# The mixers' merge and output matmuls in three rounded passes instead of full precision

## The chip, the cores and the metric

One core of one Trainium2 chip runs the whole kernel. The metric is the device time of one execution in microseconds (us).

## The reference

A decoder trunk of two layers on 256 tokens of width 1024, all in float32.

```python
for l in range(2):
    h = rmsnorm(x, norm_mix_g[l])
    z = h @ w_in[l]                        # split into the inputs of four branches and four gates
    y_a, y_b, y_c, y_d = gating(...), pool(...), rwkv7(...), ssd(...)      # each (256, 512)
    proj = einsum('btkc,kcd->btkd', [y_a, y_b, y_c, y_d], w_branch[l])
    merged = sum_k sigmoid(z_g[k]) * proj[k]
    x = x + merged @ w_out[l]
    h = rmsnorm(x, norm_ffn_g[l])
    x = x + (swiglu(h) if l == 0 else moe_swiglu(h))     # dense, or the top 2 of 8 experts
return rmsnorm(x, norm_final_g)
```

The branch `rwkv7` is a recurrence over the tokens, done in two pieces of 128 tokens, each with a triangular inverse by doubling.

## The kernel before, in words

All large weights come as one stream of chunks of 128x2048 floats (1 MB), each 16 tiles of 128x128. SyncE loads them in order into a ring of 7 slots in SBUF; a slot is loaded again when TensorE has counted its chunk in `chunks_used`. A layer's mixers have 19 chunks of input projections (`Z_UNITS`), 24 of the merge (`MERGE_CHUNKS`) and 4 of the output projection; then come 42 chunks of the dense feed-forward, or 42 for each of 8 experts.

A step of the merge has two gate chunks (h times the gate columns) and one branch chunk (`pj`, y of one branch times its projection). There are 8 steps, two a branch, in the order A, B, D, C. `sg` holds a sigmoid gate, `mg` the merged sum. The branch C (rwkv7) is a long chain of small matmuls on banks `m` with drains by VectorE and ScalarE between them. To keep TensorE busy meanwhile, the merge is cut in quarter chunks (4 tiles), and `SIDE` says how many quarters TensorE does before which stage of the chain: 8 before the lora products `cw`, 4 before `ss`, 8 before `bo`, 8 before `kt`, then for each piece of 128 tokens one at each of s1, s2, s3, at each T and X step of the 6 levels (two at X from level 2 on), one at U and one at O, then 4 before `mu` and 4 before `va`: 78 in all. `merge` does the other 18 quarters and the output. On VectorE `products` multiplies projection by gate, GpSimd adds into `mg` (L1362), and ScalarE computes the gates (`gates`, L1192). Each engine carries out its instructions strictly in the order of its own program, and waits on semaphores.

The branch chunks of C (steps 6 and 7) are the last two of the merge: they need y_C, which is ready after `mu`, `va`, a reciprocal (L1652) and five more operations (to L1661).

Two kinds of matmul occur. A full-precision one (`mm` on float32, L437) is issued as two instructions by TensorE. In the first 12 projections, the dense layer and the experts a product is done in three rounded passes (`three`): ScalarE copies the weights rounded into a buffer (`w_high`, L1201, L1213, L1246), VectorE subtracts that from the chunk and writes the rest over it in the ring (`ring_low`, L1700, L1713, L1790), and TensorE adds high x high, high x low, low x high. The normed h is split in the same way (`h_high` L1207, `h_low` L1707). Merge and output chunks and the C projections are full-precision.

The dense layer is a hardware loop of two turns of 14 chunks over gbanks in the order 0, 1, 2, 3, 0, 1, 2.

Of the kernel before, what the change touches and what calls it, by code (L numbers as in the profile page):

```python
# [48 lines left out]
RING = 7  # L49
# [9 lines left out]
NS = 12  # L59
MERGE_ORDER = [0, 1, 3, 2]  # L60
# [13 lines left out]
N_MIX = NZ + N_MERGE + N_OUT  # L74
# [14 lines left out]
for _name, _k in PP_LIST:  # L89
# [6 lines left out]
           ("off", LEVELS * P), ("count", 4 * T), ("reset", 4 * T), ("sel", H * P), ("slots", CAP), ("slot", 1)]  # L96
# [4 lines left out]
NCC = _n  # L101

# [60 lines left out]
def trunk(nc, x_in, stream, pp_in, cc_in, sw_in, rep_in, out):  # L163
    with ExitStack() as ctx:
# [6 lines left out]
        x = sb("x", [P, DT, T])  # L171
        h = sb("h", [P, DT, T])
        ring_at = -(-nc.sbuf_base // 32) * 32
        ring = sb("ring", [P, RING, CW])
        cc = sb("cc", [P, NCC])
# [7 lines left out]
        arena = sb("arena", [P, 28264])  # L183
# [34 lines left out]
        yA, yB, yC, yD = (tiles(i * 1024, 4) for i in range(4))  # L218
# [21 lines left out]
        seg1 = tiles(2048, H, P)  # L240
# [11 lines left out]
        wb = area(24168, 512)  # L252
        ub = area(24680, 512)
# [5 lines left out]
        oo = tiles(12840, 4)  # L259
# [3 lines left out]
        k2 = tiles(24168, 4)  # L263
# [3 lines left out]
        sg = area(25192, 1024).rearrange("p (b f) -> p b f", b=2)  # L267
        mg = tiles(26216, DT)

        def sg_of(step, i):  # L270
# [5 lines left out]
        gbanks = [0, 1, 2, 3, 0, 1, 2]  # L276
        gu = tiles(4096, FT)
        sil = tiles(11264, RING)
# [3 lines left out]
        h_high = part("h_high", 0, [DT, T])  # L282
        h_low = part("h_low", 2048, [DT, T])
# [39 lines left out]
        low_ready = sem("low_ready")  # L323
        v_seq = sem("v_seq")
# [10 lines left out]
            "hg_filled hg_high_ready hg_ready silu_tok hid_ready hid_turned eu_high_ready eu_ready y_ready zeroed back_filled back_drained h_split h_split_high gu_part").split()}  # L335
# [30 lines left out]
        def chunk0(l):  # L366
            return l * MIX1
# [13 lines left out]

        class Count:
# [17 lines left out]
        def _(sp):  # L400
# [5 lines left out]
            for s in range(RING):  # L406
                sp.dma_start(ring[:, s, :], stream[s]).then_inc(landed[s], 16)
                if s == 1:
                    sp.dma_start(sw[:, :], sw_in[0]).then_inc(layer_in, 16)
                    sp.dma_start(cc[:, first:NCC], cc_in[:, first:NCC]).then_inc(all_consts_in, 16)  # L410
                    sp.dma_start(rep[:, :], rep_in[0]).then_inc(layer_in, 16)
# [21 lines left out]
        def _(pe):  # L433
# [39 lines left out]
            def project(l, lo, hi):  # L473

                for n in range(lo, hi):
# [9 lines left out]
                    if name == "v":  # L485
# [7 lines left out]
                        for c in range(NCH):  # L493
                            for k in range(4):
                                tc = slice(c * P, (c + 1) * P)
                                last = three(gb(("v", c))[:, :], h_high[:, 4 * i + k, tc], h_low[:, 4 * i + k, tc],
                                             wh[:, k, :], wl[:, k, :], i == 0 and k == 0, i == 1 and k == 3)
                    else:
                        g_free(pe, l, (name, i))
                        for j in range(2):  # L500
                            for k in range(DT):
# [4 lines left out]
                                if n < NS:  # L506
                                    last = three(o, high[:, DT * j + k, :], low[:, DT * j + k, :], h_high[:, k, :], h_low[:, k, :],
# [4 lines left out]
                    if n == 1:  # L512
                        pe.wait_ge(layer_in, 32 * (l + 1))
                        pe.wait_ge(all_consts_in, 16)
# [6 lines left out]
            def mixer_d_rows(l):  # L521
# [20 lines left out]
                for i in range(4):  # L542
                    m_free(pe, l, f"row{i}")
                    for j in range(2):
                        hd = 2 * i + j
                        last = mm(mb(f"row{i}")[:, j * T:(j + 1) * T], cc[0:H, CC["sel"] + hd * P:CC["sel"] + (hd + 1) * P], d_cs)
# [197 lines left out]

            def merge_quarters(l, lo, hi):

                for n in range(lo, hi):
                    (step, unit), part = MERGE_CHUNKS[n // 4], n % 4
                    w = chunk(chunk0(l) + NZ + n // 4)
                    if unit < 2:  # L750
# [3 lines left out]
                        j = part // 2  # L754
                        for k in range(4 * (part % 2), 4 * (part % 2) + 4):
                            last = mm(gb(("gate", step, unit))[:, j * T:(j + 1) * T], w[:, DT * j + k, :], h[:, k, :],
                                      k == 0, k == DT - 1)
                    else:

                        branch = MERGE_ORDER[step // 2]  # L760
                        if part == 0:
                            if branch == 0:
                                pe.wait_ge(S["ya_ready"], NCH * (l + 1))
                            elif branch == 1:
                                m_done(pe, l, "b0")
                                m_done(pe, l, "b1")
                            elif branch == 2:
                                pe.wait_ge(S["yc_ready"], l + 1)
                            else:
# [1246 lines left out]
```

## Time and profile before

| what | value |
|---|---|
| median of 3 runs | 2276.28 us (2273.89 to 2279.42) |
| profiled execution, its own time | 2273.16 us |
| its span in the profile | 2271.3 us |
| TensorE busy | 2188.7 us, 96% |
| VectorE busy | 1426.5 us, 63% |
| ScalarE busy | 1060.5 us, 47% |
| mean granted TensorE clock | 0.977 of full |
| HBM traffic | 222 GB/s over the span |

Layer 0's mixers take from the start to 466 us, the dense layer 477 to 722, layer 1's mixers to 1183, the router and the experts the rest. A busy share is an average over all of these. An engine that waits shows as idle time, put down to the one that released it; the chain of waits walks back from the last instruction and tells which engine's work set the end.

### The profile page before, as it was taken

To read this page: it belongs to the slowest core of one execution; us is meant where nothing else is said; L and a number is where in the kernel's file an instruction comes from. 1 tells how busy PE (TensorE), PEld (TensorE's weight loads), DVE (VectorE), ACT (ScalarE), POOL (GpSimd) and SP (SyncE) were. 2 spreads that over 40 slices of the span, in tenths; PEclk is the share of its full clock that TensorE was granted. 3 is DMA by queue.
4 is the path that set the end of the run, shared out by engine and by line. 5 is a ranking of instruction groups with operands and counts; after the bars stand their busy time and mean duration, and the time that the engine had idled before them with its cause. 6 is when DMAs were issued, how large, how long until landed. Compare 5 with 4: busy or idle time off the path is not lost.

```text
span 2271.3 us, 31016 instructions
## 1 busy us (share of the span) xinstructions
PE 2188.7 (96%) x12120; PEld 1789.0 (79%) x12120; DVE 1426.5 (63%) x1355; ACT 1060.5 (47%) x898; POOL 43.8 (2%) x44
## 2 busy tenths in 40 slices
PE   7999999989998999999997999999999999999997
PEld 6988988889997988889876777777777777777775
DVE  3746331355644465533225888888888888888885
ACT  4423111133333332211113777777777777677773
POOL 0200000000000010000000000000000000000000
PEclk9999999999999999999996999999999999999998
DMA  7523212434544433322231999989898999899892
GB/s 304 184 93 130 75 56 70 170 135 178 185 184 150 149 132 110 111 75 75 75 148 47 347 348 349 368 326 366 328 368 339 356 349 346 347 351 366 329 366 101
DMA packets 69342, 504.66 MB, mean 222 GB/s; under 512 B 7696, under 2 KB 7952, under 8 KB 8208
## 3 DMA queue, kind: packets, MB, share of 16 engines
q1 hardware_dynamic: 68832, 500.57, 58.7%
q10 hardware_dynamic: 432, 2.95, 0.3%
q8 instruction: 61, 1.00, 0.2%
q14 instruction: 17, 0.14, 0.0%
HBM read 502.44 MB, written 1.05 MB: 222 GB/s over the span
## 4 chain that ended last, share of the span: by engine, by line
PE 96%; DVE 2%; ACT 1%; issue 0%; DMA 0%; SPq 0%; DVEq 0%; ACTq 0%
PE g L437 63%; PE m L437 30%; PE m L470 1%; PE m L932 1%; DVE h L1386 1%; DMA ring<-stream 0%; DVE rstd L1384 0%; DVE arena L1605 0%; ACT w_high L1201 0%; ACT L1040 0%; ACT arena L1037 0%; DVE h L1911 0%; DVE arena L1607 0%; DVE arena L1863 0%; ACT rms L1040 0%
## 5 line engine op out<-in xcount | busy, mean ns | idle before, releaser
L1790 DVE TENSOR_TENSOR ring_low<-ring,we_high 128x2048 fp32r<-128x2048 f32 x336 | 769.1, 2290 | 153.4 <-ACT we_high L1246 153.0
L1246 ACT ACTIVATE we_high<-ring 128x2048 fp32r<-128x2048 f32 x336 | 644.3, 1918 | 273.9 <-PE g L437 181.0
L437 PE MATMUL g<-we_high,hg_high 128*96 128x512 f32 x896 | 358.5, 400 | 10.3 <-DVE ring_low L1790 10.3
L437 PE MATMUL g<-ring_low,hg_high 128*96 128x512 f32 x896 | 353.9, 395 | 0.0
L437 PE MATMUL g<-we_high,hg_low 128*96 128x512 f32 x896 | 352.6, 394 | 0.0
L437 PE MATMUL g<-h,ring 128*128 128x256 f32 x1472 | 334.8, 383 | 0.0
L437 PEld LDWEIGHTS g<-h,ring 128*128 128x128 f32 x1472 | 277.3, 192 | 42.8 <-issue 7.1
L437 PE MATMUL g<-h_high,w_high 128*128 128x256 f32 x768 | 219.6, 286 | 26.8 <-DVE h_low L1707 24.7
L437 PE MATMUL m<-arena 128*128 128x128 f32 (+7 forms) x1832 | 234.0, 295 | 8.8 <-DVE arena L1605 5.8
L437 PEld LDWEIGHTS m<-arena 128*128 128x128 f32 (+3 forms) x1832 | 211.5, 186 | 29.5 <-issue 17.6
L437 PE MATMUL g<-h_high,ring_low 128*128 128x256 f32 x768 | 219.3, 286 | 0.0
L437 PE MATMUL g<-h_low,w_high 128*128 128x256 f32 x768 | 218.8, 285 | 0.0
L437 PEld LDWEIGHTS g<-we_high,hg_high 128*96 128x96 f32 x896 | 145.0, 162 | 70.8 <-DVE ring_low L1790 11.0
L437 PEld LDWEIGHTS g<-we_high,hg_low 128*96 128x96 f32 x896 | 144.6, 161 | 62.8
L437 PEld LDWEIGHTS g<-ring_low,hg_high 128*96 128x96 f32 x896 | 144.8, 162 | 59.1
L437 PE MATMUL m<-we_high,eu_high 128*96 128x512 f32 x448 | 177.3, 396 | 0.0
L437 PE MATMUL m<-we_high,eu_low 128*96 128x512 f32 x448 | 176.4, 394 | 0.0
L437 PE MATMUL m<-ring_low,eu_high 128*96 128x512 f32 x448 | 176.3, 393 | 0.0
L437 PE MATMUL g<-arena,ring 128*128 128x256 f32 x768 | 175.2, 385 | 0.0
L437 PEld LDWEIGHTS g<-h_high,w_high 128*128 128x128 f32 x768 | 147.7, 192 | 29.0 <-issue 28.9
L437 PEld LDWEIGHTS g<-arena,ring 128*128 128x128 f32 x768 | 145.9, 193 | 19.7 <-issue 0.3
L437 PEld LDWEIGHTS g<-h_low,w_high 128*128 128x128 f32 x768 | 147.6, 192 | 0.1
(242 smaller groups left out, 2209.6 us busy)
## 6 DMA issues: line engine op xcount, KB each, us to landing
ring<-stream SPq DMA_DIRECT2D x472, 1024.0 KB, 4.8
cc<-cc_in SPq DMA_DIRECT2D x1, 2352.5 KB, 15.7
sw<-sw_in SPq DMA_DIRECT2D x1, 1088.0 KB, 10.6
sw<-sw_in ACTq DMA_DIRECT2D x1, 1088.0 KB, 5.0
x<-x_in SPq DMA_DIRECT2D x1, 1024.0 KB, 4.8
out<-h ACTq DMA_DIRECT2D x1, 1024.0 KB, 3.9
rep<-rep_in SPq DMA_DIRECT2D x1, 768.0 KB, 17.2
rep<-rep_in ACTq DMA_DIRECT2D x1, 768.0 KB, 6.8
```

The source lines that it names most:

```text
L437: return pe.matmul(o, a, b, start=start, stop=stop, skip_group_check=True)
L470: last = pe.transpose(mb(stage)[:, i * P:(i + 1) * P], src, ident)
L932: last = pe.transpose(mbank[g % 2][:, j * CAP:(j + 1) * CAP], hid_tok[:, g % 2, j * P:(j + 1) * P], ident[0:CAP, 0:CAP])
L1246: A(we_high[n % 3][:, :], ring[:, slot, :], ACT.Copy).then_inc(high_ready, 1)
L1386: q.add(V.scalar_tensor_tensor(h[:, k, :], x[:, k, :], gain(k), rstd[:, :], ALU.mult, ALU.mult), done)
L1790: TT(ring_low[:, slot, :], ring[:, slot, :], we_high[n % 3][:, :], ALU.subtract).then_inc(low_ready, 1)
```

## The change

- All 28 merge and output chunks of a layer are done with `three`. A chunk is split by halves of 1024 columns: ScalarE rounds half a chunk (`z_highs`) into one of five half slots (`z_w`), VectorE subtracts it in the ring (`z_lows`), and TensorE waits in `halves` for `z_low_ready`. A half slot is free when TensorE has done the half five before (`half_free`, counted in `half_used` for first and `chunks_used` for second halves).
- ScalarE does `z_highs` inside `gates`, up to five halves ahead of the quarter at hand. VectorE has calls `z_lows(l, upto)` written between the steps of branch C, up to half 46, then two halves each in `products` 12 and 14, and the rest before the output drains.
- y of each branch and the merged sum are split as well: `y_split` and `y_lows`, `mg_high` and `mg_low`; the matmuls of `pj` wait for `y_low_ready`, those of `out` for `mg_low_ready`.
- The ring has 6 slots instead of 7. The dense layer is written out without a hardware loop and uses the banks 0 to 3 in turn.
- Buffers move: h_high has its own tensor, y_C lies in h, `sg` in `rep` (so layer 1's `rep` is loaded after the merge), `mg` partly in h. The tables `count`, `reset` and `sel` no longer stay in SBUF: pooling multiplies by a constant and by a small table `early` for the first 16 tokens, GpSimd writes `reset` with two memsets, `sel` becomes a broadcast column of the identity, and one scan becomes two.

```diff
-RING = 7
+RING = 6
+N_SLOTS = 5
+HALF = 1024
+        def half_free(eng, l, m, b):
+            at = 2 * (l * N_LATE + m) + b - N_SLOTS
+            if at >= 0:
+                before, n, half = at // (2 * N_LATE), at % (2 * N_LATE) // 2, at % 2
+                if half:
+                    eng.wait_ge(chunks_used, chunk0(before) + NZ + n + 1)
+                else:
+                    eng.wait_ge(half_used, before * N_LATE + n + 1)
@@ tensor: merge_quarters, merge
-                    w = chunk(chunk0(l) + NZ + n // 4)
+                    half, quarter = part // 2, part % 2
+                    wh, wl = halves(l, n // 4, half)      # waits for z_low_ready
...
-                            last = mm(gb(("gate", step, unit))[:, j * T:(j + 1) * T], w[:, DT * j + k, :], h[:, k, :],
+                            last = three(gb(("gate", step, unit))[:, half * T:(half + 1) * T], wh[:, quarter, k % 4, :], wl[:, quarter, k % 4, :],
+                                         h_high[:, k, :], h_low[quarter][:, k % 4, :], k == 0, k == DT - 1)
...
+                            pe.wait_ge(S["y_low_ready"], 2 * (4 * l + step // 2 + 1))
...
+                            if i == 0 and j == 0 and k % 2 == 0:
+                                pe.wait_ge(S["mg_low_ready"], 4 * l + kt // 2 + 1)
@@ tensor: the dense layer
-                with pe.Fori(0, FT // (2 * RING)) as i:
-                    for s in range(2 * RING):
+                for s in range(FT):
@@ scalar
+                act.wait_ge(S["ya_ready"], NCH * (l + 1))
+                y_split(l, 0)
                 side("cw")
...
+            def z_highs(l, upto):
+                while highs[0] < 2 * l * N_LATE + min(upto, 2 * N_LATE):
...
+                    act.wait_ge(landed[c % RING], 16 * (c // RING + 1))
+                    half_free(act, l, m, b)
+                    A(half_slot(l, m, b), half_ring(ring, l, m, b), ACT.Copy).then_inc(z_high_ready, 1)
             def gates(l, lo, hi):
+                for q4 in range(lo, hi):
+                    (step, i), part = MERGE_CHUNKS[q4 // 4], q4 % 4
+                    z_highs(l, q4 // 2 + N_SLOTS)
+                    if (step, i) == (6, 2) and part == 0:
+                        y_split(l, 2)
...
+                    if (step, i) == (2, 0):
...
+                        y_split(l, 1)
+                    if (step, i) == (4, 0):
...
+                        y_split(l, 3)
+                gates(l, SIDE_END, 12 * STEPS)
+                z_highs(l, 2 * N_MERGE + N_SLOTS)
+                for i in range(4):
+                    act.wait_ge(merged, 2 * STEPS * l + 13 + i)
+                    A(mg_high[:, 2 * i:2 * i + 2, :], mg[i], ACT.Copy).then_inc(S["mg_high_ready"], 1)
+                z_highs(l, 2 * N_LATE)
@@ vector: mixer_c, calls added between its steps
+                y_lows(l, 0)
+                z_lows(l, 5)            # before the difference L1527
+                z_lows(l, 7)            # before side cw
+                z_lows(l, 9)            # after cum_ready
+                z_lows(l, 10)           # after the ss drains
+                z_lows(l, 12)           # after the products of ss and bo
+                z_lows(l, 14)           # after the reciprocal L1581
+                z_lows(l, 16)           # after the bo drains, before side kt
+                    z_lows(l, SIDE_AT[f"s3{c}"][1] // 2 + 2)      # before the s drains
+                        z_lows(l, SIDE_AT[f"z{lv}{c}"][1] // 2 + 3)   # between the T and the X drains
+                        if (c, lv) == (1, 0):
+                            y_lows(l, 3)
+                z_lows(l, SIDE_AT["mu"][1] // 2 + 2)
+                z_lows(l, SIDE_AT["va"][1] // 2 + 3)      # before the products of mu and va
                 q.step(V.reciprocal(va[:, :, :], va[:, :, :]))
+                z_lows(l, SIDE_END // 2 + 5)
...
+                y_lows(l, 2)
+                z_lows(l, 46)
@@ vector: products and merge
                         g_done(dve, l, unit)
+                        if n in (12, 14):
+                            z_lows(l, 48 + (n - 12))
...
+                            if i == 1:
+                                for p in (n % 4 - 1, n % 4):
+                                    dve.wait_ge(S["mg_high_ready"], 4 * l + p + 1)
+                                    TT(mg_low[p][:, :, :], mg[p], mg_high[:, 2 * p:2 * p + 2, :], ALU.subtract).then_inc(S["mg_low_ready"], 1)
             def merge(l):
                 products(l, SIDE_AT["va"][1], 12 * STEPS)
+                z_lows(l, 2 * N_LATE)
```

## Rows read from the trace of the kernel before

**Rows 1.** The page: busy time of the engines, and chain by engine.
```profile
PE 2188.7 (96%) x12120; PEld 1789.0 (79%) x12120; DVE 1426.5 (63%) x1355; ACT 1060.5 (47%) x898; POOL 43.8 (2%) x44
...
PE 96%; DVE 2%; ACT 1%; issue 0%; DMA 0%; SPq 0%; DVEq 0%; ACTq 0%
```

**Rows 2.** Chain of waits, 395 to 482 us: start, duration, engine, line, count.
```profile
407.56 58.72 PE g L437 x272
```

**Rows 3.** Chain of waits, the dense layer, 480 to 722 us.
```profile
560.22 2.10 issue
562.32 80.87 PE g L437 x672
```

**Rows 4.** Groups of ScalarE by shape: tile, count, busy us, mean ns.
```profile
L1117 ACT ACTIVATE arena<-arena 128x1024 f32<-128x1024 f32 x2 | 2.1, 1043 | 0.0
```

**Rows 5.** Timelines by engine, before the recurrence: start, duration, instruction, idle before and releaser.
```profile
156.12 20.88 PE L437 MATMUL g<-h,ring 128*128 128x256 f32 x96
178.30 4.89 PE L437 MATMUL m<-arena,sw 64*128 64x256 f32 x24 [1.29 <-ACT arena L1115]
...
226.34 1.13 PE L437 MATMUL m<-arena 64*128 64x256 f32 x8 [1.40 <-DVE arena L1605]
...
943.00 1.13 PE L437 MATMUL m<-arena 64*128 64x256 f32 x8 [1.40 <-DVE arena L1605]
...
164.06 3.89 DVE L1527 TENSOR_TENSOR arena<-arena 128x3584 f32<-128x3584 f32 x1 [5.24 <-ACT arena L1059]
...
210.73 1.23 DVE L1585 TENSOR_TENSOR arena<-arena 128x1024 f32<-128x1024 f32 x1 [6.00 <-ACT small L1137]
211.87 1.22 DVE L1587 TENSOR_TENSOR arena<-arena 128x1024 f32<-128x1024 f32 x1
...
224.05 0.69 DVE L1605 TENSOR_TENSOR arena<-m,cc 128x512 f32<-128x512 f32 x1 [4.52 <-PE m L437]
...
163.23 0.60 ACT L1059 ACTIVATE arena<-g 128x512 f32<-128x512 f32 x1 [6.07 <-PE g L437]
```

**Rows 6.** Timeline of VectorE, a level with two side quarters.
```profile
367.57 0.69 DVE L1628 TENSOR_TENSOR arena<-m,arena 128x512 f32<-128x512 f32 x1 [3.73 <-PE m L437]
```

**Rows 7.** Timeline of TensorE: rounded and full-precision matmuls in turn.
```profile
750.62 0.27 PE L437 MATMUL g<-h_high,ring_low 128*128 128x256 f32 x1
750.83 3.62 PE L437 MATMUL m<-h,sw 128*8 128x256 f32 x16
754.38 0.39 PE L437 MATMUL g<-h_high,w_high 128*128 128x256 f32 x1
754.60 0.28 PE L437 MATMUL g<-h_low,w_high 128*128 128x256 f32 x1
...
1421.01 0.45 PE L437 MATMUL g<-we_high,hg_high 128*96 128x512 f32 x1
1421.30 0.39 PE L437 MATMUL g<-ring_low,hg_high 128*96 128x512 f32 x1
```

**Rows 8.** Timelines by engine, the end of the merge in layer 0.
```profile
466.10 3.62 PE L437 MATMUL m<-arena,cc 128*128 128x256 f32 x16
...
408.38 6.55 DVE L1652 RECIPROCAL arena<-arena 128x1024 f32<-128x1024 f32 x1 [5.95 <-ACT arena L1179]
...
403.08 0.60 ACT L1192 ACTIVATE arena<-g 128x512 f32<-128x512 f32 x1 [1.15 <-POOL arena L1362]
```

**Rows 9.** Windows: length, TensorE busy (instructions), granted clock, DMA share, GB/s.
```profile
470.00:472.00 2.00, 0.00 (x0) 0.94 0.29 123
...
480.00:482.00 2.00, 2.00 (x11) 0.50 0.00 0
482.00:484.00 2.00, 2.00 (x19) 1.00 0.00 0
```

**Rows 10.** Experts: SyncE's issues in a timeline, and issue to landing.
```profile
1401.29 8.67 SPq L417 DMA_DIRECT2D ring<-stream  x4
...
ring<-stream SPq DMA_DIRECT2D x67, 1024.0 KB, 4.8
```

More of the change, by code:

```diff
@@ L743, in _, with halves @@
             ys = [yA, yB, yC, yD]
+            def halves(l, m, b):
+                pe.wait_ge(z_low_ready, 2 * (l * N_LATE + m) + b + 1)
+                return half_slot(l, m, b), half_ring(ring_low, l, m, b)
             def merge_quarters(l, lo, hi):
@@ L1399, in mixer_d_decay @@
                 q.step(V.tensor_scalar(d_abs, d_dt, ahead[0:H, 0:1], -1.0, ALU.mult, ALU.mult))
-                q.step(V.tensor_tensor_scan(d_cs, cc[0:H, CC["reset"]:CC["reset"] + T], d_abs, 0.0, ALU.mult, ALU.add), S["cs_ready"])
+                for c in range(NCH):
+                    tc = slice(c * P, (c + 1) * P)
+                    ins = V.tensor_tensor_scan(d_cs[:, tc], cc[0:H, CC["ones"]:CC["ones"] + P], d_abs[:, tc], 0.0, ALU.mult, ALU.add)
+                    (q.step(ins, S["cs_ready"]) if c else q.add(ins, v_seq))
             def mixer_d_conv(l):
@@ L1659, in mixer_c, with z_lows, y_lows @@
                     m_done(dve, l, f"cg{i}")
+                z_lows(l, 44)
                 q.step(TT(oo[:, :, :], oo[:, :, :], bv[:, :, :], ALU.add))
-                q.step(TT(yC[:, :, :], oo[:, :, :], gg[:, :, :], ALU.mult), S["yc_ready"])
+                for i in range(2):
+                    two = slice(2 * i, 2 * i + 2)
+                    q.add(TT(yC[:, two, :], oo[:, two, :], gg[:, two, :], ALU.mult), S["yc_ready"])
+                y_lows(l, 2)
+                z_lows(l, 46)
+            def z_lows(l, upto):
+                while lows[0] < 2 * l * N_LATE + min(upto, 2 * N_LATE):
+                    n = lows[0] - 2 * l * N_LATE
+                    m, b = n // 2, n % 2
+                    lows[0] += 1
+                    dve.wait_ge(z_high_ready, lows[0])
+                    TT(half_ring(ring_low, l, m, b), half_ring(ring, l, m, b), half_slot(l, m, b), ALU.subtract).then_inc(z_low_ready, 1)
+            lows = [0]
+            def y_lows(l, branch):
+                for i in range(2):
+                    dve.wait_ge(S["y_high_ready"], 2 * (4 * l + MERGE_ORDER.index(branch)) + i + 1)
+                    two = slice(2 * i, 2 * i + 2)
+                    TT(y_low[branch][:, two, :], (yA, yB, yC, yD)[branch][:, two, :], y_high[:, two, :], ALU.subtract).then_inc(S["y_low_ready"], 1)
             def products(l, lo, hi):
```

241 lines of the change are left out of this document (135 added, 106 removed).

## The prediction

> **What bounds the kernel now.** I read the page first: TensorE is busy 96% of the span, and the chain that ended last runs through it for 96% [rows 1]. So the question is how fast TensorE's work is and who can make it wait. The changed matmuls are the merge and output chunks: 28 chunks of 16 weight tiles in each of two layers, 896 tiles. Today a tile is a full-precision product of two instructions; in the longest run of them in the chain of waits 272 take 58.72 us, 0.216 each, 0.432 a tile [rows 2]. The dense stage already does three rounded passes: 672 instructions in 80.87 us, 0.1203 each, 0.361 a tile [rows 3]. The saving is 0.071 us a tile: 0.29 us a quarter chunk (1.73 to 1.44), and 64 us for all 896 if nothing else waits.
>
> By the Trainium skill (TensorE: Matmul & The Clock Gate, Back-to-back issue gap) a matmul of 256 columns follows the last after 109 ns; a tile would then take 0.33 us, and the saving be 94 us. The trace has 0.1203, so the row is used.
>
> **What is added.** Each of 56 half chunks a layer now needs a rounding copy on ScalarE and a subtraction on VectorE, of 128x1024 each. Nearest rows: 1.04 us on ScalarE [rows 4], 1.23 on VectorE, where the next one starts 1.14 after the last [rows 5]. That is 64 us of VectorE and some 55 of ScalarE a layer; the y and merged tiles add twelve pairs of 128x512 at 0.69 and 0.60 [rows 5]. In total VectorE has room (63% busy over the span), but each engine works in the order of its code, and the new instructions stand between links of the chain. So I follow layer 0 in three stretches. Layer 1 is the same 716.66 us later (226.34 and 943.00) [rows 5].
>
> **Stretch 1, from the last projection to the recurrence** [all from rows 5]. TensorE ends the projections at 163.0 (156.12 and 32 instructions) and today goes straight on with merge work; 28 quarters of it cover VectorE's preparation. After the change the first quarter waits: evacuation to 163.8, two roundings of y to 165.0, first rounding of weights 166.0, first subtraction 167.3. Idle 4.3. VectorE does y_lows(0) and five z_lows before its difference: 171.9 instead of 164.1; then 3.9 and 5.6 of mixing (to 181.5), tanh and sigmoid, and the lora matmuls start at 182.4 instead of 178.30. From there VectorE is the chain, in the order of its code: w_log scaled at 185.4, scan and sums 5.9, two z_lows, k2 2.6, the ss drain 1.3, one z_low, 3.6 for bonus, marker and products (202.3), two z_lows behind ScalarE's root and rounding (205.1), reciprocal 6.6, two z_lows, kk 1.2: 215.2. Today it is at this point at 210.73, after 6.00 us of waiting; that wait hides the other half of what is added. The five operations up to ab_ready take 5.9: 221.1; bonus drains 1.3. Then z_lows(16): ScalarE makes halves 14 and 15 only in its side "kt", after ab_ready and two drains, so their subtractions end at 226.9, and two products put the first drain of n (L1605) at 228.5 instead of 224.05. TensorE's pair of matmuls behind it comes at 230.7 instead of 226.34, after 6.4 us idle. Four quarters there give back 1.15; the clock (below) takes 1.8. Balance +5.0 us.
>
> **Stretch 2, the recurrence.** In a level with two side quarters VectorE has nothing to do for 3.73 us between draining T and draining X [rows 6]. With quicker quarters that gap is some 3.1 us, and 1.5 where a level has one quarter. One or two subtractions (1.2 or 2.4) are put into it; where two meet the short gap they are late by 0.8, which the next quarter hides. ScalarE waits only for halves used before its own step. So here TensorE stays the bound: 38 quarters save 10.9. y_lows(3), at level 0 of the second chunk, adds 1.3 to a short gap; I charge 1.0. If this cover were gone, a subtraction on the chain would cost its 1.2.
> Changing between rounded and full-precision matmuls: around the dt product (8 weight columns) the rounded instruction is followed after 0.21, the sixteen take 3.55 and the first rounded one is followed after 0.22, against 0.12, 3.46 and 0.12: +0.28 a round trip. After the expert transposes (128 wide) the first rounded one is followed after 0.29 instead of 0.23: +0.06 [rows 7]. With 40 interruptions a layer the bounds are 0 and 11 us; the weights here are wide like the transposes, so I take 0.06, 2.4 us. Balance -7.5.
>
> **Stretch 3, the end of the merge.** Today the va matmuls end at 407.56; eight quarters before them give 2.3: 405.2. On VectorE three z_lows stand before the products of step 5, so the gate (6,0), today at 403.08 behind GpSimd's sum, comes at 405.2; the gate, a rounding, the table load and two roots (0.6, 1.0, 1.3, 1.6) put the reciprocal at 409.6, today 408.38 [rows 8]. Halves 42 and 43 are subtracted only behind its 6.55: at 417.3 and 418.5. TensorE has finished half 41 at 413.8: idle 3.5. Next, ScalarE rounds y_C behind the gate (7,1) and half 48, which both wait for the end of half 43; then come y_lows(2) and half 44: 4.7 idle. Today TensorE reaches pj 6 at 424.8 without a wait; that cover is what goes. Halves 46 and 47 are subtracted only in products(12), which waits for all of chunk 22: 2.0. Halves 48 and 49 stand behind mg_low 0 and 1, these behind ScalarE's half 52, which needs the slot of half 47: 4.8. Half 50 stands behind mg_low 2 and 3: 1.2. From 417.3 on, 14 halves of 2.89 give 457.8, the four later waits 12.7, three clock drops 5.4: 475.9. Today 466.28. Balance +9.6.
>
> **The clock.** TensorE's last matmul before the norm ends at 469.7 [rows 8]. The granted clock was 0.94 in 470 to 472, 0.50 (1.2 GHz) in 480 to 482, when it had been back at work since 477.26, and 1.00 (2.4 GHz) from 482 [rows 9]. At 1.2 GHz 256 columns take 0.213 us instead of 0.1203. I take 4.1 us low, which costs 1.8 us an idle. Today only the norms and the router have such gaps; the short idles of 1.29 and 1.40 us in rows 5 brought no drop. I take a drop for each idle of 3.5 us or more: the one that counts in stretch 1 (before 167.3 another is hidden by the wait for 182.4) and three in stretch 3. Bounds: none, 7.2 us a layer less; all at the length of 477.26 to 482, 1 us a layer more.
>
> **The rest.** Unrolling the dense stage removes the 2.10 us at its loop's turn [rows 3]. The ring of six: in the experts a slot is issued every 2.9 us (three periods in 8.67) and landing takes 4.8 [rows 10]; ScalarE runs three chunks ahead, so a chunk has three periods, 8.7 us, instead of four: nothing, and about one period once if that margin failed. Half chunks free a slot with their second half, as a chunk does today. The smaller constants and their extra transfer land before anyone waits; GpSimd's two reset memsets and its rewritten pooling run long before they are asked for; rep for layer 1 is fetched behind the merge and used in layer 1; the broadcast identity column in place of "sel" and the split scan keep their counts: each nothing, at most 1 us.
>
> **Sum.** A layer: 5.0 - 7.5 + 9.6 = +7.1; two, less 2.1: +12.1. Against the profiled execution's own 2273.16 (span 2271.3) this is 2285.3. The median of the runs shown is 3.1 higher, so 2288.
>
> **Rivals.** (A) TensorE stays the only bound. For it: 96% busy, and VectorE idle for 3.73 us of each long level. All 64 us and the 2.1: 2210. Against: the waits of stretches 1 and 3 follow from the order of the code. Chance 0.10. The Trainium skill (Perfetto Trace Analysis, Identifying the Most-Contended Engine) says to relieve the engine with the highest occupancy; followed without looking at the order, that is this rival, and the rows of stretch 2 agree with it, those of 1 and 3 do not.
> (B) The same waits, but the clock stays up (14.4 less) and half of the four later idles of stretch 3 is absorbed (12.7 less): 2261. For it: these idles are near 4 us, where today's drops have over 7. Against: each is longer than the 2.3 us from 469.7 to 472. Chance 0.27, between 2245 and 2279.
> (C) On the other side: each round trip between precisions costs the 0.28 of the dt row; 80 times 0.22 more is 17.6: 2306. Its point of decision is 0.09 a trip: from there the change costs time even with the clock up all through (7.1 less 7.2 and 1.05 a layer, and 40 times 0.03). For it: rows 7. Against: no such loss into 128 columns. Chance 0.10.
> Forecast 0.53, its own range 2279 to 2300.
>
> **Numbers.** Within 0.2% of 2276.3 (2271.7 to 2280.9) a measurement of this kernel cannot tell from no change. Faster: A and two thirds of B, 0.29; same 0.14, the rest of B and the forecast's lower edge; slower 0.57. Range 2250 to 2308: it leaves out A and the far ends.
>
> **What would show it.** In the chain of waits, pieces of VectorE and ScalarE in 163 to 231 and 413 to 456, where today almost only TensorE stands. TensorE idle 3 to 5 us before the first merge quarter, before pj 6 and before out 0, released by ring_low or y_low, with a granted clock of 0.50 behind it. A level of two side quarters and one shorter by 0.9 us. A dense stage without its 2.10. I am wrong if the first drain of n stays within 2 us of today's, or if out 0 follows pj 7 without a gap.

## The result and the profile after

The changed kernel takes 2281.96 us (median of 13 runs, 2281.71 to 2287.89), the kernel before 2274.52 (13 runs of its own, 2270.68 to 2279.61): a ratio of 1.003, with a 95% interval of 1.0021 to 1.0039. It is slower by some 7 us. The profiled execution has a span of 2280.6 us, 9.3 longer, and its mean granted TensorE clock is 0.961 instead of 0.977.

The page first, its lines on busy time and the chain. TensorE is busy for 44 us less than in [rows 1], VectorE for 136 us more and ScalarE for 121 more. The chain no longer runs through TensorE alone: its share fell from 96% to 55%, with gaps that the profile can't follow.

```profile
PE 2145.0 (94%) x13016; PEld 1790.1 (78%) x13016; DVE 1562.3 (69%) x1495; ACT 1181.5 (52%) x1033; POOL 49.3 (2%) x56
...
PE 55%; DVE 4%; issue 1%; ACT 1%; POOL 0%; DVEq 0%; ACTq 0%
```

Next the waits of TensorE over the span (engine and line, what it waited for, us in total, times, longest). The first and the fourth line are new.

```profile
PE g L480 <- DVE ring_low L1778: 39.2, 12, 4.9
PE g L480 <- DVE h_low L1838: 24.0, 3, 9.3
PE m L480 <- ACT arena L1073: 12.6, 3, 7.8
PE m L480 <- ACT arena L1185: 12.3, 2, 6.3
```

Two of these waits stand ahead of the recurrence: the one ahead of the first merge quarter, which waits for the first subtracted half, and the one ahead of the score matmuls, which wait for a bank that ScalarE drains at L1185. Timelines of the kernel after, layer 0, with the instructions that answer to [rows 5] (last evacuation on ScalarE, halves and first drain of n on VectorE, TensorE):

```profile
162.23 0.60 ACT L1095 ACTIVATE arena<-g 128x512 f32<-128x512 f32 x1 [6.07 <-PE g L480]
163.76 4.84 ACT L1228 ACTIVATE z_w<-ring 128x1024 fp32r<-128x1024 f32 x5
...
164.84 5.77 DVE L1778 TENSOR_TENSOR ring_low<-ring,z_w 128x1024 fp32r<-128x1024 f32 x5
226.87 0.68 DVE L1698 TENSOR_TENSOR arena<-m,cc 128x512 f32<-128x512 f32 x1
...
180.89 4.89 PE L480 MATMUL m<-arena,sw 64*128 64x256 f32 x24 [1.60 <-ACT arena L1153]
230.27 3.79 PE L480 MATMUL m<-arena 64*128 64x256 f32 x16 [6.03 <-ACT arena L1185]
```

These 16 score matmuls are two groups of eight. In the kernel before, the first group ran at 223.85 and the second, the line at 226.34 in [rows 5], waited for VectorE's first drain of n. In the kernel after, both stand behind ScalarE's drain, and the second group starts at 232.11 (after, then the first group before, each group seen by itself):

```profile
232.11 1.95 PE L480 MATMUL m<-arena 64*128 64x256 f32 x8
```
```profile
223.85 1.09 PE L437 MATMUL m<-arena 64*128 64x256 f32 x8
```

The end of the merge, the same view of TensorE and VectorE, against [rows 2, 8]. TensorE stands still ahead of half 42 (412.39), of the branch chunk of step 7 (434.89) and of the first output chunk (445.83); ahead of the first branch chunk of C at 424.47 it waited 4.61 as well. The last addition to x comes at 471.86.

```profile
412.39 0.38 PE L480 MATMUL g<-h_high,z_w 128*128 128x256 f32 x1 [3.59 <-DVE ring_low L1778]
424.47 0.58 PE L480 MATMUL g<-y_high,z_w 128*128 128x256 f32 x1 [4.61 <-DVE ring_low L1778]
434.89 0.39 PE L480 MATMUL g<-y_high,z_w 128*128 128x256 f32 x1 [2.04 <-DVE ring_low L1778]
445.83 0.58 PE L480 MATMUL g<-mg_high,z_w 128*128 128x256 f32 x1 [4.92 <-DVE ring_low L1778]
451.42 0.39 PE L480 MATMUL g<-mg_high,z_w 128*128 128x256 f32 x1 [0.47 <-DVE ring_low L1778]
...
404.52 6.55 DVE L1754 RECIPROCAL arena<-arena 128x1024 f32<-128x1024 f32 x1 [4.86 <-ACT arena L1217]
471.86 0.69 DVE L1823 TENSOR_TENSOR x<-g,x 128x512 f32<-128x512 f32 x1 [4.88 <-PE g L480]
```

Windows behind two of these idles (length, TensorE busy with its instructions, weight loads, VectorE, ScalarE, GpSimd, granted clock, DMA share, GB/s). TensorE is back at work all through them, at half the clock (1.2 GHz), as in the first line at work of [rows 9].

```profile
424.47:429.00 4.53, 4.53 (x21) 4.53 (x22) 1.08 (x1) 0.00 (x0) 0.00 (x0) 0.50 0.02 4
446.00:450.00 4.00, 4.00 (x19) 4.00 (x20) 3.87 (x6) 1.26 (x2) 0.00 (x0) 0.50 0.00 0
```

With the same marks in both traces the whole difference can be laid out. The marks are the first matmul of a layer, the last evacuation of its projections, the second group of its score matmuls (226.34 before, 232.11 after), the end of the O matmuls of the second piece, and the last addition to x.

| stretch, us | before | after | change | predicted |
|---|---|---|---|---|
| layer 0, start to last evacuation | 163.23 | 162.23 | -1.0 | 0 |
| 1, to the second group of score matmuls, layer 0 / 1 | 63.11 / 63.11 | 69.88 / 70.16 | +6.8 / +7.0 | +5.0 each |
| 2, the recurrence, layer 0 / 1 | 163.68 / 163.71 | 153.08 / 152.92 | -10.6 / -10.8 | -7.5 each |
| 3, the end of the merge, layer 0 / 1 | 76.28 / 76.28 | 86.67 / 86.55 | +10.4 / +10.3 | +9.6 each |
| norm, dense layer, norm | 271.05 | 267.04 | -4.0 | -2.1 |
| layer 1, first matmul to last evacuation | 142.54 | 143.72 | +1.2 | 0 |
| router, experts, final norm | 1088.31 | 1088.35 | 0.0 | 0 |
| span | 2271.3 | 2280.6 | +9.3 | +12.1 |

### The profile page after: what moved, and what is told of

It reads as the page before. It is cut to its first block, busy times and chain, and to the rows that moved or that the text cites. A ratio compares the mean times of both kernels' runs of the same rounds, so it can differ in the third digit from the quotient of the medians.

```text
span 2280.6 us, 33009 instructions
## 1 busy us (share of the span) xinstructions
PE 2145.0 (94%) x13016; PEld 1790.1 (78%) x13016; DVE 1562.3 (69%) x1495; ACT 1181.5 (52%) x1033; POOL 49.3 (2%) x56
## 4 chain that ended last, share of the span: by engine, by line
PE 55%; DVE 4%; issue 1%; ACT 1%; POOL 0%; DVEq 0%; ACTq 0%
PE g L480 33%; PE m L480 21%; DVE ring_low L1778 1%; PE m L968 1%; PE m L513 0%; DVE arena L1754 0%; DVE arena L1672 0%; ACT z_w L1228 0%; DVE h L1467 0%; DVE h L2040 0%; DVE arena L1992 0%; DVE small L1994 0%; DVE y_low L1787 0%; DVE ring_low L1919 0%; DVE small L1455 0%
## 5 line engine op out<-in xcount | busy, mean ns | idle before, releaser
L480 PE MATMUL g<-we_high,hg_high 128*96 128x512 f32 x896 | 358.6, 400 | 10.3 <-DVE ring_low L1919 10.3
L480 PE MATMUL g<-h_high,ring_low 128*128 128x256 f32 x1280 | 366.2, 286 | 0.0
L480 PE MATMUL m<-arena 128*128 128x128 f32 (+7 forms) x1832 | 239.8, 302 | 20.4 <-ACT arena L1185 12.3
L480 PEld LDWEIGHTS g<-h_high,ring_low 128*128 128x128 f32 x1280 | 249.7, 195 | 0.0
L480 PEld LDWEIGHTS g<-ring_low,hg_high 128*96 128x96 f32 x896 | 144.8, 162 | 59.1
L1228 ACT ACTIVATE z_w<-ring 128x1024 fp32r<-128x1024 f32 x112 | 115.8, 1054 | 127.5 <-PE g L480 127.5
L1778 DVE TENSOR_TENSOR ring_low<-ring,z_w 128x1024 fp32r<-128x1024 f32 x112 | 132.4, 1220 | 53.1 <-ACT arena L1210 39.5
L480 PE MATMUL g<-h_high,z_w 128*128 128x256 f32 x512 | 153.1, 299 | 15.0 <-DVE ring_low L1778 15.0
```

Of the source, the lines that this page charges most:

```text
L480: return pe.matmul(o, a, b, start=start, stop=stop, skip_group_check=True)
L1228: A(half_slot(l, m, b), half_ring(ring, l, m, b), ACT.Copy).then_inc(z_high_ready, 1)
L1778: TT(half_ring(ring_low, l, m, b), half_ring(ring, l, m, b), half_slot(l, m, b), ALU.subtract).then_inc(z_low_ready, 1)
```

## The experiments

In what follows "after" is the changed kernel; each ratio is against runs of the kernel before on the same chip. A time "below after" compares medians of different chips, on which the kernel before has medians of 2274.5, 2276.5, 2278.7 and 2275.8 us, so such a difference is uncertain by a few us; by the ratios it is 26 us instead of 26.5 in the first experiment, for instance, and 19 instead of 16 in the one with two passes.

**The order at the end of the merge.** Nothing is computed differently; small instructions of VectorE and ScalarE change places.

```diff
 vector, mixer_c
                 side("mu", "va")
+                z_lows(l, 43)
 ...
+                z_lows(l, 45)
                 y_lows(l, 2)
-                z_lows(l, 46)
+                z_lows(l, 48)
 vector, products
-                        if n in (12, 14):
-                            z_lows(l, 48 + (n - 12))
 ...                                       # n == 13, ahead of mg_low and behind it
+                                    z_lows(l, 50)
+                                    z_lows(l, 52)
 scalar
-                    if (step, i) == (6, 2) and part == 0:
-                        y_split(l, 2)
+                    if (step, i) == (7, 1):          # behind its sigmoid
+                        y_split(l, 2)
-                gates(l, SIDE_END, 12 * STEPS)
+                gates(l, SIDE_END, 12 * STEPS - 2)   # mg_high 0 and 1 next, then the rest, then 2 and 3
```

> The changed kernel with another order of the small instructions in the end of each layer's merge, nothing else: half 42 is subtracted while VectorE waits for the square roots; the split of the recurrent mixer's output is issued by ScalarE right behind the last gate and not behind one more rounding; halves 44 to 49 and 50, 51 are subtracted in VectorE's free time ahead of the wait that they are needed at; the first two roundings of the merged tiles come ahead of two roundings of weights. Theory (stretch 3 is lost to waits that the order makes): TensorE's idles of 4.6, 2.0 and 4.9 us ahead of the last two projections and the first output chunk go, the projection of the recurrent mixer starts at 419.9 instead of 424.5, and the last add of x comes about 11.5 us earlier in each layer: 2282 - 23 = 2259 us. Rival (the waits only stand in for a chain of reciprocal, affine, split and products that would end last anyway, and the clock falls as before): at most the 4.6 us a layer, 2273 us. Rival (the stretch is paid in TensorE time, not in waits): no change, 2282 us.

Measured: 2255.46 us (2254.82 to 2257.70, 6 runs), ratio 0.9915 (0.990 to 0.993). That is 26.5 below after, a little more than the theory's 23. TensorE's timeline of this kernel has two idles left in the stretch; branch chunk 7 and the first output chunk (at 436.25, without an idle) follow at once. From the va matmuls (400.67) to the last addition to x it takes 59.26 us, in after 73.49 (398.37 to 471.86).

```profile
400.67 1.89 PE L480 MATMUL m<-arena,cc 128*128 128x256 f32 x8
...
414.68 0.39 PE L480 MATMUL g<-h_high,z_w 128*128 128x256 f32 x1 [0.75 <-DVE ring_low L1782]
422.21 0.55 PE L480 MATMUL g<-y_high,z_w 128*128 128x256 f32 x1 [4.40 <-issue]
436.25 0.36 PE L480 MATMUL g<-mg_high,z_w 128*128 128x256 f32 x1
```

TensorE's own time over the two stretches tells idles and clock apart (same columns as the windows above: length, TensorE busy, weight loads, VectorE, ScalarE, GpSimd, granted clock, DMA share, GB/s; after first, then this kernel). The same 419 matmuls keep it busy for 57.85 us and for 53.92. So of the 14.2 us, 10.3 are idles, and 3.9 are the half clock that had stood behind two of them.

```profile
398.37:471.86 73.49, 57.85 (x419) 56.62 (x418) 40.39 (x47) 27.19 (x32) 2.56 (x2) 0.88 0.41 151
400.67:459.93 59.26, 53.92 (x419) 52.98 (x418) 40.29 (x47) 27.41 (x32) 2.56 (x2) 0.94 0.49 186
```

So what stretch 3 lost was lost to the order, and both rivals fall. One idle of 4.4 us is left. The profile names no releaser for it; it ends when VectorE has made `y_low` (422.10), the last link behind the reciprocal and the split of y_C.

**The start alone, and both.**

```diff
 scalar
-                evacuate(l, Z_UNITS[18:])
+                evacuate(l, Z_UNITS[18:-1])
+                act.wait_ge(S["ya_ready"], NCH * (l + 1))
+                y_split(l, 0)
+                z_highs(l, N_SLOTS)
+                evacuate(l, Z_UNITS[-1:])
 ...                                       # and in mixer_c
-                act.wait_ge(S["ya_ready"], NCH * (l + 1))
-                y_split(l, 0)
```

> The changed kernel, in which only the split of the first mixer's output and the first five roundings and subtractions of weight halves are moved ahead of the last evacuation of the projections, into the 6 us in which ScalarE and VectorE both wait for TensorE. Theory (stretch 1 is lost to the 7.1 us that VectorE spends on them ahead of the mixing of the recurrent mixer's inputs): the idle of 3.9 us ahead of the first merge quarter goes, the mixing begins near 163.5 instead of 170.5, and the first drain of the recurrence comes 4 us earlier in each layer (7 at most): 2282 - 8 = 2274 us. Rival (the eleven later halves in the preparation, 13 us of VectorE, are what delays it, and the first five only filled time): under 1 us a layer, 2281 us. Rival (TensorE's own merge work sets the stretch once it need not wait): 2 us a layer, 2278 us.

Measured: 2276.63 us (2272.36 to 2278.74, 12 runs), ratio 1.0001 (0.999 to 1.0013), 5.3 below after, between the theory's 8 and the last rival's 4. The trace shows the theory's step and its limit. TensorE's idle ahead of the first quarter is gone. But ScalarE's roundings run until 165.2, so the last evacuation itself starts 0.3 us late, and VectorE's subtractions run until 168.0, where the mixing could begin at 166.1: 58.9 us from the last evacuation (165.47) to the first drain of n (224.33), in after 64.64, in the kernel before 60.82. In layer 1 it is 60.73, so stretch 1 gains 5.8 and 3.9 us, as the theory has it. But in this profile the projections ahead of it take 3.2 and 2.8 us longer than in after, and the granted clock in them is lower (0.85 over 100 to 123 us, in after 1.00); that takes back much of the gain. The score matmuls still wait 6.12.

```profile
165.47 0.60 ACT L1095 ACTIVATE arena<-g 128x512 f32<-128x512 f32 x1 [0.30 <-PE g L480]
...
162.31 5.76 DVE L1780 TENSOR_TENSOR ring_low<-ring,z_w 128x1024 fp32r<-128x1024 f32 x5
224.33 0.68 DVE L1700 TENSOR_TENSOR arena<-m,cc 128x512 f32<-128x512 f32 x1
...
227.73 1.65 PE L480 MATMUL m<-arena 64*128 64x256 f32 x6 [6.12 <-ACT arena L1183]
```

> The changed kernel with both reorderings, that of the end of the merge and that of the first five halves. Theory (two separate losses): the sum of the two gains, 2282 - 23 - 8 = 2251 us, which is 23 us below the kernel before. Rival (what is gained at the start is given back in the recurrence, since the chain there waits for halves): 2259 us, as the end alone. Rival (the gains of both are small): above 2270 us.

Measured: 2244.71 us (2242.69 to 2250.56, 5 runs), ratio 0.987 (0.9851 to 0.9889). That is 37 us below after, where the two alone gave 26.5 and 5.3: the gains add, with 5 us more than their sum, about the spread of such runs.

**The entry of the recurrence.** What was left of stretch 1 is an idle that is 6.94 us in this last kernel. ScalarE drains `kt` and `nt` only behind gate (2,0), which waits for VectorE's products, and behind a table load and the split of y_B.

```diff
 scalar, mixer_c
-                side("kt")
+                gates(l, SIDE_AT["kt"][0], SIDE_AT["kt"][1] - 1)
                 for i, name in enumerate(("kt", "nt")):
 ...
+                gates(l, SIDE_AT["kt"][1] - 1, SIDE_AT["kt"][1])
 vector, mixer_c
-                z_lows(l, 16)
                 side("kt")
+                z_lows(l, 16)
```

> The kernel with both reorderings, and one more at the entry of the recurrence: ScalarE drains the banks of kt and nt ahead of the sigmoid of gate (2,0), its table load and the split of the second mixer's output instead of behind them, and VectorE makes the two products ahead of subtracting halves 14 and 15. In the kernel with both reorderings TensorE stands idle for 6.9 us ahead of the first score matmul (222.1 to 229.1), for a bank that ScalarE drains at 228; the kernel before has 1.4 us there. Theory (this wait is of the order alone): the first drain of the recurrence comes 1.7 us earlier in each layer and the score matmuls up to 3 us: 2245 - 3 to 6 = 2240 us, with the idle under 4 us. Rival (the recurrence's chain on VectorE sets the pace there, so TensorE's idle is cover for it): no gain, 2245 us. Rival (the second mixer's split now comes too late for its first quarter): 2246 us or more, with a new idle near 235.

Measured: 2238.34 us (2238.12 to 2243.33, 5 runs), ratio 0.9838 (0.9817 to 0.9859), 6.4 below the kernel with both. The score matmuls start after 2.68 us of idle, and the first drain of n comes 57.3 us behind the last evacuation (162.48 to 219.75), now earlier than in the kernel before (59.1 in layer 1, where the kernel before has 60.8 as well). What stretch 1 lost was order too.

```profile
162.48 0.60 ACT L1095 ACTIVATE arena<-g 128x512 f32<-128x512 f32 x1 [0.30 <-PE g L480]
219.75 0.68 DVE L1703 TENSOR_TENSOR arena<-m,cc 128x512 f32<-128x512 f32 x1
...
221.39 2.23 PE L480 MATMUL m<-arena 64*128 64x256 f32 x11 [2.68 <-ACT arena L1183]
```

**Waits or clock.** After, with matmuls on constants ahead of the four waits.

```diff
+            def warm(l, count):
+                m_done(pe, l, "va0")
+                for _ in range(count):
+                    mm(mb("va0")[:, 0:T], heads, cc[:, CC["off"]:CC["off"] + T], True, True)
 ...
+                    if n in {84: 7, 88: 9, 92: 3}:       # and 10 ahead of output chunk 0
+                        warm(l, {84: 7, 88: 9, 92: 3}[n])
```

> The changed kernel, with matmuls on constants that fill TensorE's four idles in the end of each merge and nothing else (7, 9, 3 and 10 float32 matmuls of 256 columns into a bank that is free there, 0.43 us each, issued just ahead of the waits for halves 42, 44, 46 and 48; their results are not used). It keeps the waits and takes away only the clock that falls behind them. Theory (the waits cost twice: themselves, and the half clock in which 425 to 430 and 446 to 450 us run): 2 to 2.5 us behind each of two waits, 4.5 us a layer, 2282 - 9 = 2273 us, with the granted clock of 385 to 472 us near 1.0 instead of 0.90. Rival (the drops lie inside waits and cost nothing): 2282 us. Rival (the added matmuls outlast the idles): 2284 us or more.

Measured: 2275.83 us (2271.60 to 2280.61, 12 runs), ratio 0.9994 (0.9982 to 1.0006), 6 below after (8 by the two ratios). The window that stood at 0.66 stands at 1.00:

```profile
420.00:430.00 10.00, 5.53 (x26) 5.53 (x27) 3.56 (x4) 2.47 (x4) 0.00 (x0) 0.66 0.29 107
```
```profile
420.00:425.00 5.00, 4.72 (x26) 3.89 (x24) 3.14 (x5) 2.58 (x4) 0.00 (x0) 1.00 0.56 202
425.00:430.00 5.00, 4.55 (x38) 4.55 (x39) 1.53 (x2) 1.06 (x1) 0.00 (x0) 1.00 0.03 11
```

The first is after, the other two are this kernel. From the va matmuls to the last addition to x it takes 71.11 us in layer 0 (400.87 to 471.98) and 69.62 in layer 1 (1116.49 to 1186.11), against 73.49 and 73.37: 2.4 and 3.8 us, not 4.5. In layer 1 the clock stays at 1.00 all through, in layer 0 it falls once more behind 451. Part of what the clock gives comes back as a wait: the second output half now waits 2.44 us instead of 0.47. The waits, not the clock, are the larger part of stretch 3: the new order took 10.3 us of idles out of it.

> The kernel with all three reorderings, and 9 matmuls on constants in the one idle that is left in the end of the merge (4.4 us, ahead of the projection of the recurrent mixer's output). Theory (a half clock of some 5 us follows it in each layer): 2 to 2.5 us a layer less than without them, 2240 - 5 = 2235 us. Rival (the clock behind it would be back in time anyway, or the added matmuls delay the projection): as without them, 2240 us.

Measured: 2234.49 us (2228.56 to 2238.31, 5 runs), ratio 0.9816 (0.9792 to 0.984): the three reorderings and 9 such matmuls in the one idle left. It is the fastest of all, 47 us below after and 1.8% below the kernel before. From the va matmuls to the last addition the profile has 57.03 us (389.61 to 446.64) instead of 58.35, and in layer 1 57.01 instead of 58.29. Against the kernel without them (lowest 2238.12) the gain of 4 us is at the edge of what so few runs tell, and the trace accounts for 2.6 of it.

**What bounds the recurrence.** After, with two passes instead of three in its 42 side quarters.

```diff
+            def two(o, high, low, x_high, x_low, start, stop):
+                mm(o, high, x_high, start, False)
+                return mm(o, high, x_low, False, stop)
 ...
+                    passes = two if SIDE_AT["s10"][0] <= n < SIDE_AT["mu"][0] else three
```

> The changed kernel, with only two of the three passes (the product of low weights with the rounded input is left out) in the 42 side quarters between the first score matmul and the recurrent mixer's second output; the roundings, subtractions and waits for them all stay. Leaves out: that part of the gate and merge products. It asks what bounds the recurrence after the change. Theory (TensorE is the bound there, with cover left): 42 quarters of 4 passes of 0.118 us are 19.8 us a layer, 40 in all, 2282 - 40 = 2242 us, with the stretch from the first drain of n to the va matmuls down from 171.5 to 152. Rival (the new subtractions have used up VectorE's gap, and its chain takes over): less than half of it, 2262 us or more, with the drains of VectorE no longer waiting for TensorE. Rival (the change of precision costs more than the passes): 2275 us.

Measured: 2265.99 us (2254.96 to 2270.80, 10 runs), ratio 0.9946 (0.9926 to 0.9966). 16 us less, not 40: by the total, the first rival. The trace says otherwise. In layer 0, up to the W matmuls of the second piece (350.41) it is 120.6 us from the first drain of n (229.78), in after 137.5 (364.39 from 226.87): 16.9 us saved of the 18.9 that 40 quarters hold, and TensorE waits for VectorE nowhere longer than 1.5 us. Then the clock falls, and stays down for some 27 us, in after and before for some 7 (the first three windows are this kernel, the next two after, the last two before):

```profile
340.00:352.00 12.00, 12.00 (x102) 11.66 (x101) 8.39 (x11) 4.17 (x6) 0.05 (x1) 1.00 0.43 150
352.00:380.00 28.00, 28.00 (x113) 21.44 (x114) 1.46 (x2) 3.74 (x6) 0.00 (x0) 0.53 0.03 12
380.00:390.00 10.00, 10.00 (x75) 9.79 (x75) 2.90 (x6) 2.34 (x3) 0.00 (x0) 0.94 0.30 107
```
```profile
368.00:372.00 4.00, 4.00 (x16) 3.44 (x16) 0.00 (x0) 1.01 (x3) 0.00 (x0) 0.55 0.00 0
372.00:376.00 4.00, 4.00 (x25) 4.00 (x23) 0.00 (x0) 0.59 (x1) 0.00 (x0) 0.59 0.00 0
```
```profile
372.00:376.00 4.00, 4.00 (x15) 3.27 (x15) 0.00 (x0) 0.66 (x2) 0.00 (x0) 0.60 0.01 4
376.00:380.00 4.00, 4.00 (x17) 3.46 (x16) 0.00 (x0) 0.00 (x0) 0.00 (x0) 0.55 0.00 0
```

28 us at 0.53 lose 13.2 us, the 8 us of after 3.4. To the va matmuls 8.9 us are saved (162.6 against 171.5), and with the 9.8 of the clock 18.7 of the 19.8 expected. Layer 1 does the same: 120.9 us from the first drain of n to the W matmuls (137.7 in after), 162.9 to the va matmuls (171.6), and the same clock in between:

```profile
1062.00:1090.00 28.00, 28.00 (x113) 21.44 (x114) 1.47 (x2) 3.74 (x6) 0.00 (x0) 0.53 0.03 13
```

Behind the va matmuls the end of the merge takes 74.7 us in both layers, 1.2 and 1.3 more than in after. So TensorE is the bound of the recurrence, and half of the gain went back to the clock. Why the clock stays down so long is open.

**The dense layer.** The kernel before with its loop written out, as in the change, with everything else kept; its profile was taken twice.

```diff
-                with pe.Fori(0, FT // (2 * RING)) as i:
-                    for s in range(2 * RING):
+                for s in range(FT):
 ...
-                                last = three(gbank[gbanks[s % RING]][:, j * T:(j + 1) * T], high[s % 2][:, DT * j + k, :],
+                            last = three(gbank[s % 4][:, j * T:(j + 1) * T], high[s % 2][:, DT * j + k, :],
```

> The kernel before with one part of the change alone: the loop of the dense layer's gate and up chunks written out, with bank n modulo 4, the ring of seven and the places of all buffers kept. Theory of the prediction (only the gap of 2.10 us between the two turns goes): 2274.5 - 2.1 = 2272.4 us, dense stretch from 260.1 to 258.0 us. Rival (the loop also makes each pass slower, 0.1199 us a pass in it against 0.1178 us in the changed kernel, over 1344 passes): 2274.5 - 4.0 = 2270.5 us, dense stretch 256.1 us. If the slower pass comes of where the buffers or the ring lie, the stretch stays at 258.0 us.

> The kernel before with the dense layer's loop written out, once more, for its profile. In its first profile the passes came every 0.1203 us in the gate and up chunks and 0.1200 us in the down chunks; in the kernel before 0.1200 and 0.1185, in the changed kernel 0.1178 and 0.1185. If the spacing belongs to the program, this profile shows 0.1203 and 0.1200 again and a dense stretch of 258.6 us. If it differs from execution to execution, it shows another pair, and what the dense stretch gained beyond the 2.10 us of the loop's turn is no effect of the change.

Measured: 2271.98 us (2264.75 to 2276.90, 12 runs), ratio 0.9975 (0.9961 to 0.9989), then once 2266.28. The pause is gone in both. The dense layer with the norm behind it takes 258.62 us in the first profile and 257.79 in the second, in the kernel before 260.09, in after 256.08. In the chain of waits the gate and up chunks (1344 passes) and the down chunks (672) are, in the first profile:

```profile
480.10 163.46 PE g L437 x1344
643.56 80.65 PE m L437 x672
```

and in the second:

```profile
477.51 163.63 PE g L437 x1344
641.14 79.65 PE m L437 x672
```

In after the first down pass comes at 644.57, 161.75 us behind the first gate pass at 482.82; in the kernel before this is 165.76 us (477.26 to 643.02) with the pause of 2.10 [rows 3]. So the loop's turn is worth 1.5 to 2.3 us, and the down chunks differ by 1.0 us between two executions of one kernel. The other 1.7 to 2.5 us are passes that follow each other quicker in the gate and up chunks of after; the loop is not their cause, since they are slow in both profiles without it. Nor is it chance of one execution: in the eight profiles of after and of its variants the dense layer with its norm takes 255.2 to 256.6 us, in the three with the buffers of the kernel before 257.8 to 260.1. Which of the moved buffers, or the ring, makes the difference was not tried. The runs of this kernel are 2.5 to 8.9 us below those of the kernel before (the interval of the ratio), which can't tell the theory's 2.1 us from the rival's 4.0.

## Why the prediction was right

The forecast was 2288 and slower; the median is 2282, the span's change 9.3 where the sum had 12.1 (the median of the kernel before is 1.8 us lower in 13 runs than in the 3 that the forecast started from). Each of the three stretches moved in the direction given, for the reason given. That the sum came so close is in part luck: over two layers stretch 1 cost 3.8 us more than forecast and stretch 3 1.5 more, stretch 2 gave 6.4 more and the dense layer 1.9 more.

- **Stretch 1**, +5.0 predicted, +6.8 and +7.0 measured. The idle ahead of the first quarter is 3.92 (4.3), the one ahead of the score matmuls 6.03 (6.4), VectorE's first drain of n 226.87 (228.5, less the 1.0 by which the layer starts sooner). What was too small is the time to the second group of score matmuls: 4.4 us later by the prediction, 6.8 in the trace. (The rest of the 5.0, the clock's 1.8 less 1.15 for four quarters, lies behind this mark.) The prediction put the idle down to VectorE's order and let only the second group wait for it. What TensorE waits for last is ScalarE's drain at L1185, which is chained to VectorE's products; the first group waits for it too, and takes 1.84 us at half clock (230.27 to 232.11) before the second can start. It named the right delay and the wrong last link. Moving the first halves and moving that drain each recovered a part.
- **Stretch 2**, -7.5 predicted, -10.6 and -10.8 measured. A side quarter and the sixteen chain matmuls behind it take 3.20 us in after (245.46 to 248.66) instead of 3.51 (239.60 to 243.11 in the kernel before):

```profile
245.46 0.37 PE L480 MATMUL g<-y_high,z_w 128*128 128x256 f32 x1
...
246.96 1.95 PE L480 MATMUL m<-arena 128*128 128x128 f32 x16
248.66 0.36 PE L480 MATMUL g<-y_high,z_w 128*128 128x256 f32 x1
```
```profile
239.60 1.89 PE L437 MATMUL g<-arena,ring 128*128 128x256 f32 x8
241.33 1.95 PE L437 MATMUL m<-arena 128*128 128x128 f32 x16
243.11 1.89 PE L437 MATMUL g<-arena,ring 128*128 128x256 f32 x8
```

  Eight full-precision instructions at 0.216 are 1.73 us, twelve passes at 0.118 are 1.42: 0.31 less, all of what is measured. The quarter itself is 0.08 longer than its passes (1.50), and the chain's sixteen are 0.08 shorter than before (1.70 against 1.78), so a round trip between the precisions costs next to nothing where 0.06 was taken, and a pass 0.118 where 0.1203 was. The 42 quarters behind the mark give 13.0 us (the prediction booked four of them in stretch 1); half clock from 232.11 to 235.31 costs 1.6, and y_lows(3) 0.6, where 1.0 was charged: the quarter and block from 321.33 take 4.68 us, others of that form 4.08. ScalarE's roundings take 58 us a layer and not the 55 of the prediction, which had no effect.

  The 109 ns that the Trainium skill gives for 256 columns (TensorE: Matmul & The Clock Gate, Back-to-back issue gap) is nearer to 0.118 than to 0.1203, and still not what any stretch here shows.
- **Stretch 3**, +9.6 predicted, +10.4 and +10.3 measured. Idles of 3.5, 4.7, 2.0, 4.8 and 1.2 were predicted; 3.59, 4.61, 2.04, 4.92 and 0.47 came, 0.6 us less in all. The term that was too small is the clock, charged with 5.4 us. TensorE is busy for 57.85 us from 398.37 to 471.86; the kernel with all reorderings and nine added matmuls of 0.43, at a clock of 1.00, needs 55.54 for the same work and those nine, so some 6 us are the half clock. Keeping the clock up gave back only 2.4 and 3.8, since part of it turned into waits.
- **The dense layer**, -2.1 predicted, -4.0 measured. This term was too small: the turn was read rightly, the quicker passes were not foreseen, and what makes them quicker is open.
- **Projections**, 0 predicted, -1.0 and +1.2 measured. No change of the code is known to explain either; the granted clock fits both. In layer 0 it is 0.57 over 113 to 117 us in the kernel before and 1.00 over 100 to 120 in after; in layer 1 it is 0.57 over 830 to 834 before and 0.57 over 832 to 840 after. Each time that is a difference of some 1.7 us. Runs of the kernel before differ by 9 us among themselves.
- **The ring of six** cost nothing in the experts: 1088.3 us from the last addition of layer 1 to the end in both.

**The rivals.** A (TensorE the only bound, 2210) did not happen, but three reorderings take the same arithmetic to 2238: of the 72 us between the changed kernel and A, 44 were the order of the code. This also bears on the rule that the prediction weighed against it, to relieve the engine with the highest occupancy (the Trainium skill, Perfetto Trace Analysis, Identifying the Most-Contended Engine): the relief paid in the stretch where nobody else stood in the way, and was lost in the other two until their order was mended. B (clock up, half of the idles absorbed, 2261) fell on both counts. C (0.28 a round trip, 2306) fell: a round trip costs 0.03 at most.

## What to carry to other kernels

When the busiest engine gets faster, its old work no longer covers the preparation on the others: list every instruction that now feeds it, with the time at which it is ready and the time at which its place in its own engine's order lets it run, since the distance between these two was most of the loss here (43 of the 47 us between the changed kernel and the best version came from moving instructions whose inputs were ready earlier). Put the feeding work of a stage into the idle time ahead of the last link that starts it, and drains that release a bank ahead of anything that waits for another engine.

## What the runs showed of the hardware

- The granted clock fell to 0.50 with no idle ahead of it. It did so in layer 0 of all eleven profiles, in the W matmuls of the second piece, 64-column products one behind the other; TensorE counts as busy for all of 372 to 380 us in the kernel before. The prediction tied drops to idles of 3.5 us and more. The clock stayed down for some 7 to 10 us, and for some 27 in the kernel with two passes, in both of its layers.
- A rounded pass of 256 columns followed the last after some 0.118 us in the gate and up chunks of after and after 0.120 in those of the kernel before, with the same shapes; and the same down chunks of one kernel took 80.65 and 79.65 us in two executions.
- Changing between rounded and full-precision matmuls and back costs at most 0.03 us with weights 128 wide (3.20 us against 3.51 for a quarter and the chain's sixteen), far less than the 0.28 around the 8-column weights [rows 7].
